# The first product of the second modulation half on GpSimd instead of VectorE, in a one-core decoder trunk

## The reference

```
cond = silu(c)
mod = cond @ ada_w[layer] + ada_b[layer]            # 1024 -> 6 * 1024
sh_m, sc_m, g_m, sh_f, sc_f, g_f = split(mod, 6)
h = rmsnorm(x, gn[0]) * (1.0 + sc_m) + sh_m
y = stick_breaking(h, w_in, w_out)                  # layer 0; layer 1: latent attention
x = x + g_m * rmsnorm(y, gn[1])
h = rmsnorm(x, gn[2]) * (1.0 + sc_f) + sh_f
y = swiglu(h) or moe(h)                             # layer 0; layer 1: top 2 of 8 experts
x = x + g_f * rmsnorm(y, gn[3])
```

## Time and profile before

| | us |
|---|---|
| median of three runs | 822.77 |
| lowest and highest | 822.61, 823.52 |
| the profiled execution | 823.02 |
| its span in the trace | 821.2 |

### The profile page before, as it was taken

The page is one execution under the profiler, slowest core; times in us unless marked ns, Lnnn a source line. Parts: engine busy times, 40 slices in busy tenths (PEclk is TensorE's granted clock), DMA queues, the critical chain, the costliest instruction groups (busy, mean ns, idle before and its releaser), DMA issues.

```text
span 821.2 us, 12488 instructions
## 1 busy us (share of the span) xinstructions
PE 799.5 (97%) x4682; PEld 710.8 (87%) x4682; DVE 688.4 (84%) x587; ACT 542.4 (66%) x575; POOL 31.2 (4%) x48
## 2 busy tenths in 40 slices
PE   4999999999999999999999999999999999999995
PEld 4999788999999888999888888888888888888884
DVE  4988787789889876778469898898989898898998
ACT  5346846544343434756388797968789797878875
POOL 1000000000000000000012000000000000000120
PEclk9999999999999999999999999999999999999998
DMA  8999686499899997399929999999999999999992
GB/s 335 422 416 363 235 303 235 172 371 370 324 369 395 395 356 272 128 347 420 421 94 365 427 394 413 355 422 366 397 404 351 418 351 425 354 409 397 362 415 79
DMA packets 46794, 284.31 MB, mean 346 GB/s; under 512 B 6029, under 2 KB 6032, under 8 KB 21157
## 3 DMA queue, kind: packets, MB, share of 16 engines
q1 hardware_dynamic: 41002, 269.06, 83.9%
q0 software_dynamic: 3584, 12.60, 3.9%
q10 hardware_dynamic: 2170, 2.13, 0.8%
HBM read 258.09 MB, written 25.17 MB: 345 GB/s over the span
## 4 chain that ended last, share of the span: by engine, by line
PE 84%; DVE 5%; issue 4%; ACT 3%; DMA 3%; POOL 1%; SPq 0%; DVEq 0%; ACTq 0%; POOLq 0%
PE ps L2339 8%; PE ps L2335 8%; PE ps L2334 8%; PE ps L1835 7%; PE ps L1839 7%; PE ps L1843 7%; PE ps L2350 4%; PE ps L2351 4%; PE ps L2355 4%; PE ps L1771 3%; PE ps L1772 3%; PE ps L1773 3%; PE ps L1790 1%; PE ps L1791 1%; PE ps L1795 1%
## 5 line engine op out<-in xcount | busy, mean ns | idle before, releaser
L1591 DVE TENSOR_TENSOR w_lo<-ring,w_hi 128x2048 fp32r<-128x2048 f32 (+1 forms) x96 | 210.0, 2201 | 29.7 <-ACT w_hi L934 29.4
L588 ACT ACTIVATE w_hi<-ring 128x2048 fp32r<-128x2048 f32 (+1 forms) x56 | 106.4, 1900 | 138.0 <-PE ps L1843 80.8
L934 ACT ACTIVATE w_hi<-ring 128x2048 fp32r<-128x2048 f32 (+1 forms) x96 | 174.8, 1839 | 8.8 <-PE ps L2339 8.8
L1099 DVE TENSOR_TENSOR w_lo<-ring,w_hi 128x2048 fp32r<-128x2048 f32 (+1 forms) x56 | 127.1, 2271 | 39.1 <-ACT w_hi L588 38.9
L1835 PE MATMUL ps<-hT_hi,w_hi 128*128 128x256 f32 x480 | 118.0, 282 | 0.0
L1843 PE MATMUL ps<-hT_hi,w_lo 128*128 128x256 f32 x480 | 117.2, 281 | 0.0
L1839 PE MATMUL ps<-hT_lo,w_hi 128*128 128x256 f32 x480 | 117.2, 281 | 0.0
L1591 DVE TENSOR_TENSOR m_lo<-ring,m_hi 128x1536 fp32r<-128x1536 f32 (+1 forms) x48 | 92.7, 1931 | 2.3 <-ACT m_hi L934 1.9
L2335 PE MATMUL ps<-w_hi,xe_lo 128*128 128x512 f32 (+1 forms) x256 | 92.3, 376 | 0.0
L2334 PE MATMUL ps<-w_hi,xe_hi 128*128 128x512 f32 (+1 forms) x224 | 85.1, 380 | 0.0
L1835 PEld LDWEIGHTS ps<-hT_hi,w_hi 128*128 128x128 f32 x480 | 83.2, 189 | 0.5 <-issue 0.5
(11 more groups left out here) (401 smaller groups left out, 1452.9 us busy)
## 6 DMA issues: line engine op xcount, KB each, us to landing
ring<-in_moe_w_gu SPq DMA_DIRECT2D x64, 1024.0 KB, 7.3
ring<-in_ada_w SPq DMA_DIRECT2D x48, 1024.0 KB, 6.9
ring<-in_moe_w_down SPq DMA_DIRECT2D x32, 1024.0 KB, 7.5
ring<-in_moe_w_gu SPq DMA_DIRECT2D x32, 768.0 KB, 8.0
ring<-in_ffn_w_gu SPq DMA_DIRECT2D x22, 1024.0 KB, 6.5
ring<-in_sb_w_in SPq DMA_DIRECT2D x12, 1024.0 KB, 9.1
ring<-in_moe_w_down SPq DMA_DIRECT2D x16, 768.0 KB, 7.0
ring<-in_ffn_w_down SPq DMA_DIRECT2D x11, 1024.0 KB, 6.7
```

The costliest lines, as they stand in the source:

```text
L588: act.activation(split_of(m)[0][:, 0:cols_n], ring[n % R][:, 0:cols_n], ACT.Copy).then_inc(hi_done, 1)
L934: act.activation(m_hi[k % NB][:, 0:n_c], ring[(N0 + k) % R][:, 0:n_c], ACT.Copy).then_inc(hi_done, 1)
L1099: dve.tensor_tensor(split_of(m)[1][:, 0:cols_n], ring[n % R][:, 0:cols_n], split_of(m)[0][:, 0:cols_n].bitcast(F32), ALU.subtract).then_in ...
L1591: dve.tensor_tensor(m_lo[k % NB][:, 0:n_c], ring[(N0 + k) % R][:, 0:n_c], m_hi[k % NB][:, 0:n_c].bitcast(F32), ALU.subtract).then_inc(free ...
```

## The change

GpSimd, behind the clearing of `blank`, waits for `cond` and for piece 5, multiplies both blocks of the piece by their column of `cond` (the first into `acc`, the second in place in the ring slot), waits for its own two results and for `freed` at 5, adds the two, and counts piece 5 as freed. VectorE loses its `ada_pair()` for piece 5 and waits in its place until `freed` stands at 6; then it goes on with `lo(1)`.

```diff
@@ -344,6 +344,7 @@
+        pool_half = sem("pool_half")
@@ -508,6 +509,16 @@
             pool.memset(blank[:, :], 0.0).then_inc(blank_ok, 1)
             pool.wait_ge(blank_ok, 1)
 
+            n = ada_no[0, 0, 4]
+            piece, dst = paired_piece(n, 0, 4)
+            pool.wait_ge(cond_ok, 1)
+            wait_piece(pool, n)
+            pool.tensor_scalar(dst, piece[:, 0], cond[:, 0:1], None, ALU.mult).then_inc(pool_half, 1)
+            pool.tensor_scalar(piece[:, 1], piece[:, 1], cond[:, 1:2], None, ALU.mult).then_inc(pool_half, 1)
+            pool.wait_ge(pool_half, 2)
+            pool.wait_ge(freed, n)
+            pool.tensor_tensor(dst, dst, piece[:, 1], ALU.add).then_inc(freed, 1)
+
@@ -1315,7 +1326,9 @@
             dve.memset(warm_out[:, 15:16], 0.0).then_inc(freed, 1)
             pieces[0] += 1
             modulated(0, 4, second_half=False)
-            ada_pair()
+            assert stream[pieces[0]][1] == (0, 0, 4)
+            pieces[0] += 1
+            dve.wait_ge(freed, pieces[0])
             lo(1)
             ada_pair()
             lo(2)
```

## The result

| | us |
|---|---|
| kernel before, median of 14 runs | 822.02 (821.33 to 823.52) |
| changed kernel, median of 14 runs | 824.72 (824.04 to 825.04) |
| ratio, with its 95% interval | 1.0030 (1.0023 to 1.0037) |
| the profiled execution of the changed kernel | 824.15, span 822.6 |

The change makes the kernel slower by 2.7 us by the medians. The 14 runs of the kernel before form two groups of seven, 821.33 to 821.49 and 822.56 to 823.52, and their median lies in the gap between them; against the one group the loss is 3.3 us, against the other 2.0. The three runs that the prediction started from, with the median 822.77, are all of the upper group.

The account below looks back on a forecast made before the run. TensorE, busy 799.5 of 821.2 us, was taken as the bound. Removing its 0.3 us wait before L1963, with nothing charged for GpSimd's work, took the median from 822.77 to 822.5 us; range 820.8 to 824.6.

Parts of the forecast that it names:

- the price of GpSimd's multiplication: Each multiplication of 1024 columns on piece 5 was to take 1.05 us, between 0.95 and 1.13.
- The addition: GpSimd's sum of the two blocks was to take 2.1 us, at most 2.3, running from 25.0 to 27.1.
- The fifth rival: GpSimd's addition ends between 29.3 and 30.3, VectorE gets no lead, TensorE's wait stays: 822.8 us; chance 0.03.
- its next link: At L1843, first reader of the low half at 32.60, TensorE would stand only if `lo(1)` began later than 30.3.
- VectorE keeps 0.5 of 1.98 us: Before `lo(1)`, 0.5 us of the removed work becomes lead and 1.4 us a new wait for ScalarE.
- The direct gain: At the reduction L1963 TensorE loses its wait for `acc`, 0.3 us, carried on to the end.
- I take nothing: GpSimd's work beside VectorE's `scale` and `hT_lo`, 22.6 to 28 us, costs VectorE nothing; upper end a full block by each operation.
- The third rival: Engines exclude each other at the dearest, TensorE stands near 26 us, its clock falls after: +2.8, 825.6 us; chance 0.12.
- The fourth rival: The clock fall at 45.4 us vanishes with the idling before L1963, giving 1.7 us beside the 0.3: 820.8; chance 0.10.
- the lateness rival: Another name for the fifth rival: GpSimd's three operations take over 6.7 us after the landing; 822.8 us, chance 0.03.

Follow-up runs that it names:

- m1_micro: A separate kernel without the computation, timing GpSimd's operations alone and beside VectorE's stream; one profiled run: multiplication of 1024 columns 2.84 us alone.
- x8_memsets: Changed kernel with piece 5's sums left out; GpSimd clears its own tile nine times and VectorE waits for that; 824.42 against 821.66 us before, ratio 1.0032.
- x1: Changed kernel with piece 5's sums left out altogether, VectorE only counting the piece as freed; 821.45 against 821.47 us before, ratio 1.0002.
- x2b: Second series of x2: GpSimd makes only the first multiplication, VectorE adds the second block; 821.21 against 822.73 us before, ratio 0.9985.
- x2: Changed kernel with only the first multiplication of piece 5 on GpSimd, VectorE adding the second block; 821.14 against 821.47 us before, ratio 0.9998.
- x5: Changed kernel, GpSimd's addition not waiting for `freed`, VectorE waiting for it only behind `lo(1)`; 824.85 against 821.52 us before, ratio 1.0045.
- x6: Changed kernel with GpSimd's two multiplications written as `tensor_tensor` against a broadcast column; 822.78 against 821.52 us before, ratio 1.0015.
- x3: Changed kernel with seven filler products on TensorE in front of its wait for `lo(1)`; 825.06 against 821.47 us before, ratio 1.0034.

## Why the prediction was wrong

I predicted 822.5 us, -0.3 against the median shown, with a range to 824.6; measured were 824.72 and a loss of 2.7 us.

**The step that failed** is the price of GpSimd's multiplication, "between 0.95 and 1.13 us; I take 1.05". It is 3.50 and 3.19 us. The rows it was taken from, a select of 128 columns and a memset of 1024, were GpSimd's own, but other operations, and I called the range closed at both ends though neither row was a multiplication. m1_micro has the size: 2.84 us alone. The addition, 2.1 with an upper bound of 2.3, took 2.41, a small miss; the estimate of 2.25 us from the Trainium skill ("GPSIMD Engine Reference", section "Elementwise — side-by-side cycle accounting") was nearer, and the trace, 2.34 us alone, agrees with it within 4%. Together the end is at 31.94 in place of 27.1: 4.6 us from the multiplications, 0.3 from the addition.

**The mechanism was written down and mispriced.** The fifth rival, GpSimd late, had a chance of 0.03, and its condition, "over 6.7 us after the landing", came true with 9.3. I also had its next link: TensorE "would stand only if `lo(1)` began later than 30.3". It began at 31.97, and TensorE stood 1.77 us, by that rule 1.67. But I closed the rival at 30.3 and gave it 822.8, where it should have been carried on: VectorE's queue 2.2 us late, the reduction as late, 822.8 + 2.2 = 825.0. x8_memsets shows that this alone, without a single read by GpSimd, makes the loss.

**What held.** VectorE keeps 0.5 of 1.98 us, the rest becomes a wait for ScalarE (1.38 us in x1, 1.4 predicted). TensorE's products begin where they did. The direct gain, had GpSimd been in time, is 0.45 us at the reduction (16.18 to 16.20 behind the first product in place of 16.65); I had taken the wait of 0.3 us alone, from the end of the last product's row. But the rows overlap: the next one starts 0.12 us behind the start of the product before it and doesn't wait for its end. The last product and the reduction, first in the kernel before, then in x2b:

```profile
42.00 0.28 PE L1843 MATMUL ps<-hT_hi,w_lo 128*128 128x256 f32 x1
42.57 1.92 PE L1963 MATMUL ps<-ones,acc 128*128 128x1 f32 x16 [0.29 <-DVE acc L1140]
```

```profile
41.91 0.28 PE L1856 MATMUL ps<-hT_hi,w_lo 128*128 128x256 f32 x1
42.02 1.86 PE L1976 MATMUL ps<-ones,acc 128*128 128x1 f32 x16
```

So 0.57 becomes 0.11 us. The main group of x2 lies 0.2 to 0.3 us lower.

**The contention.** "I take nothing" was nearly right for the change as it is: `scale` 0.32 for 0.17 and the last `hT_lo` 0.73 for 0.43 us, neither of which TensorE waited for. But it was right by the kind of operation and not by the reasons I gave, which is luck. With two inputs on both engines they hold each other up, in both directions: GpSimd's addition 4.10 us beside `w_lo` (x5), VectorE's `scale` 1.10 us beside GpSimd's broadcast multiplication (x6). That is the Trainium skill's exclusive pair of ports ("SBUF — State Buffer", section "SBUF: two separate sides"), and in x5 and x6 the traces agree with it. For GpSimd's `tensor_scalar` they agree only in part: `scale`, at 24.20, did not stand until that operation's end at 26.25.

**The clock.** The third rival had the right sign and nearly the right time, 825.6, by another cause, so that is luck too: TensorE didn't stand near 26 us, but at 32.5. The fourth rival's mechanism, the fall at 45 us going away with the idling before the reduction, had 0.10 and is what happens in x2, where it is most of the gain, 1.3 us in the runs that would have had it. In the changed kernel it went the other way: one fall came in either profile, at 35 or at 48 us.

## What to carry to other kernels

An operation that an engine hasn't done in the trace has no price from its other operations, and no upper bound either: time it by itself first (m1_micro would have told), or leave the range open upwards, and carry the lateness rival through to the end of the chain instead of stopping it where it begins to hurt. When work is moved to an engine with time to spare, count from when its input lands to when its result is due (here 22.6 to 27.9 or 29.3), and move only what fits: one multiplication of 3.5 us gave the whole usable lead and a kernel that is a little faster than the one before in one of two series (0.9985, 0.9974 to 0.9996) and can't be told from it in the other (0.9998, 0.9989 to 1.0008), three operations of 9.2 us gave a loss. In this kernel two-input operations on GpSimd and on VectorE at the same time held each other up (x5, x6), and are best kept apart.

## What the runs showed of the hardware that I had not expected

GpSimd's `tensor_scalar` of 128x1024 f32 takes 2.84 us with a column and 2.77 with an immediate, more than its `tensor_tensor` against a broadcast column of the same size (1.89 us) or against a second tensor (2.34 us).

A fall of TensorE's clock need not cost what it takes. From 35 to 38.4 us the changed kernel ran at 0.53 and x3 at 1.00, but x3 reached the reduction only 0.6 us sooner, because there it waited for VectorE. Behind the reduction, where TensorE waits for nothing, a fall costs its full 1.3 us, and so x3's profile, with its fall there, is the longer of the two.

The group of runs near 818.8 us is another thing again. The profile of x2_one_mult fell into it: from GpSimd's bias at 175.04 to that at 264.79 it took 89.75 us, where every other profile took 91.9. That is 2.1 of the 2.8 us between this profile and that of x2b. In it products follow each other by 0.113 us (0.34 / 3) and not by 0.118 (0.47 / 4); the timeline of x2_one_mult, then that of the kernel before:

```profile
222.67 0.28 PE L1852 MATMUL ps<-hT_lo,w_hi 128*128 128x256 f32 x1
222.78 0.28 PE L1856 MATMUL ps<-hT_hi,w_lo 128*128 128x256 f32 x1
222.89 0.28 PE L1848 MATMUL ps<-hT_hi,w_hi 128*128 128x256 f32 x1
223.01 0.28 PE L1852 MATMUL ps<-hT_lo,w_hi 128*128 128x256 f32 x1
```

```profile
223.46 0.28 PE L1835 MATMUL ps<-hT_hi,w_hi 128*128 128x256 f32 x1
...
223.93 0.28 PE L1839 MATMUL ps<-hT_lo,w_hi 128*128 128x256 f32 x1
```

The granted clock is 1.00 in both. What sets the spacing stays open; no run here was made for it.
